# Down projection of the second feed-forward block: from one per pair of tiles to seven block products behind all tiles, in a decoder layer on one core

## The reference

```python
def swiglu(x, w_gate, w_up, w_down):
    return (jax.nn.silu(x @ w_gate) * (x @ w_up)) @ w_down

    h = swiglu(rmsnorm(x, ffn1_pre_norm[i]), ffn1_w_gate[i], ffn1_w_up[i], ffn1_w_down[i])
    x = x + MACARON_WEIGHT * rmsnorm(h, ffn1_post_norm[i])
    h = hybrid_mixer(rmsnorm(x, mix_pre_norm[i]), cos, sin, w_in[i], conv_w[i], conv_b[i],
                     dt_bias[i], a_log[i], d_skip[i], ssm_norm[i], w_out[i])
    x = x + rmsnorm(h, mix_post_norm[i])
    h = swiglu(rmsnorm(x, ffn2_pre_norm[i]), ffn2_w_gate[i], ffn2_w_up[i], ffn2_w_down[i])
    x = x + MACARON_WEIGHT * rmsnorm(h, ffn2_post_norm[i])
```

## Time and profile before

| | |
|---|---|
| median of three runs | 2281.05 us |
| lowest and highest of the three | 2279.21 and 2282.74 us |
| span of the profiled execution | 2278.5 us |
| TensorE busy in it | 2238.8 us, 98% |
| VectorE busy | 1698.9 us, 75% |
| ScalarE busy | 917.6 us, 40% |
| GpSimd busy | 230.4 us, 10% |

### The profile page before, as it was taken

How to read it: one execution, slowest core, us unless ns; L and a number is a source line. 1 busy time by engine, 2 the same in 40 slices (tenths; PEclk the granted TensorE clock), 3 DMA queues, 4 the chain that set the end, 5 groups by cost and what they waited for, 6 DMA issues and landing times. The chain is left out here.

```text
span 2278.5 us, 29774 instructions
## 1 busy us (share of the span) xinstructions
PE 2238.8 (98%) x10460; PEld 1835.5 (81%) x10460; DVE 1698.9 (75%) x2547; ACT 917.6 (40%) x1614; POOL 230.4 (10%) x213
## 2 busy tenths in 40 slices
PE   9999999999999999999999999999999999999998
PEld 7888888888877877778788777788888888888887
DVE  8877777777759787786666686879877777777767
ACT  6322222222334576777531774225332222222224
POOL 0000000000000344443100226100000000000000
PEclk9999999999999999999999999999999999999999
DMA  4111111111323001101221135133121111111123
GB/s 161 56 51 47 50 55 55 55 50 38 124 100 114 20 10 38 38 10 56 75 67 54 65 121 175 56 121 111 38 70 50 47 55 55 55 55 52 41 87 135
DMA packets 54748, 154.65 MB, mean 68 GB/s; under 512 B 6144, under 2 KB 8192, under 8 KB 52608
## 3 DMA queue, kind: packets, MB, share of 16 engines
q1 hardware_dynamic: 54656, 153.46, 20.0%
HBM read 132.14 MB, written 21.30 MB: 67 GB/s over the span
## 5 line engine op out<-in xcount | busy, mean ns | idle before, releaser
L1094 DVE TENSOR_TENSOR acc<-psum,acc 128x512 f32<-128x512 f32 x288 | 197.8, 690 | 161.0 <-PE psum L583 158.2
L710 ACT CAST t_hi<-t_raw 128x512 fp32r<-128x512 f32 x144 | 89.6, 622 | 319.9 <-DVE t_raw L900 303.0
L583 PE MATMUL psum<-act_hi,tile_lo 128*128 128x512 f32 x544 | 211.9, 389 | 0.0
L582 PE MATMUL psum<-act_lo,tile_hi 128*128 128x512 f32 x544 | 211.9, 389 | 0.0
L581 PE MATMUL psum<-act_hi,tile_hi 128*128 128x512 f32 x544 | 211.9, 389 | 0.0
L732 ACT ACTIVATE sum<-sum 128x512 f32<-128x512 f32 x72 | 45.6, 633 | 245.1 <-DVE sum L1048 150.4
L2097 PE MATMUL psum<-norm_hi,tile_hi 128*128 128x512 f32 x320 | 129.2, 404 | 1.8 <-DVE z_scaled L2505 1.8
L2414 DVE TENSOR_TENSOR probs_t_lo<-psum,probs_t_hi 128x512 fp32r<-128x512 f32 x144 | 97.1, 685 | 39.2 <-ACT probs_t_hi L2331 38.3
L2099 PE MATMUL psum<-norm_hi,tile_lo 128*128 128x512 f32 x320 | 125.1, 391 | 0.0
L2098 PE MATMUL psum<-norm_lo,tile_hi 128*128 128x512 f32 x320 | 125.0, 391 | 0.0
L581 PEld LDWEIGHTS psum<-act_hi,tile_hi 128*128 128x128 f32 x544 | 102.2, 188 | 21.2
(11 more groups left out here) (436 smaller groups left out, 5870.2 us busy)
## 6 DMA issues: line engine op xcount, KB each, us to landing
tile_lo_raw<-in_d SPq DMA_DIRECT2D x40, 512.0 KB, 4.3
gate_raw<-in_gu SPq DMA_DIRECT2D x36, 512.0 KB, 3.8
up_raw<-in_gu SPq DMA_DIRECT2D x72, 256.0 KB, 3.7
raw_tile<-in_w_att SPq DMA_DIRECT2D x28, 512.0 KB, 3.7
x_scratch<-acc SPq DMA_DIRECT2D x32, 256.0 KB, 2.1
cum_rows<-cum_scratch SPq DMA_DIRECT2D x8, 1024.0 KB, 4.7
raw_tile<-in_w_out SPq DMA_DIRECT2D x15, 512.0 KB, 3.6
gate_up_lo_raw<-in_gu SPq DMA_DIRECT2D x7, 1024.0 KB, 6.1
```

The lines of the kernel that those rows point to most:

```text
L582: pe.matmul(o, w_h[:, s, d, :], a_l[:, s, x], start=False, stop=False)
L583: mm = pe.matmul(o, w_l[:, s, d, :], a_h[:, s, x], start=False, stop=(s == 1))
L710: act.copy(to, of).then_inc(sem(p + "_t_hi"), 1)
L1094: v.tensor_tensor(x, banks(4 + d % 4), x, ALU.add).then_inc(sem(p + "_acc"), 1)
```

## The change

Only the second block changes. The first two tiles stay plain; all 20 others become seven tiles, where the last two were plain. No tile pair has a down projection behind it. The product silu(gate) x up of a tile goes to a staging buffer (`stage`), from there by a 512 KB store to a DRAM scratch (`acts`), 22 times.

Behind all tiles, the whole down projection is one 2x2 block product: the 22 inner tiles in two groups of 11 (rows 0 to 10 and 11 to 21), the 8 output blocks in two groups of 4, with the two token halves on the other side. Seven products (0 to 6 in the code) x 11 steps x 4 blocks x 3 = 924 matmuls. A step is 12 matmuls. The activations come back from DRAM in nine transfers, the weights by steps in 256 KB transfers, two where a product's weights are a sum. GpSimd forms the weight sums (`down_w_sum`, 55 of 128x512, for products 0, 1, 3, 4 and 6), VectorE the activation sums (`down_b_sum`, 55, products 1, 2, 3, 5 and 6), ScalarE the casts `w_hi` and `b_hi`, VectorE the rests `w_lo` and `b_lo` (77 of each). There are 11 slots of operands; slot k is free for product m once TensorE is through step k of product m-1. ScalarE puts 16 results into `down_sums`, VectorE adds 32. The norm and the residual behind it stay; their steps and those of the products are ordered by a new `end_plan`.

```diff
             wait(pe, p + "_up", 4)
             seven_pe(pe, p, 1, 0, sums=True)
             seven_pe(pe, p, 1, 1)
+            if p == "f2":
+                with pe.Fori(2, LAST_PAIR + 1) as i:
+                    seven_pe(pe, p, i, 0)
+                    seven_pe(pe, p, i, 1)
+                return
...
-                v.tensor_tensor(e1[:], e1[:], e4[:], ALU.mult).then_inc(sem(p + "_read"), 1)
+                if p == "f2":
+                    v.wait_ge(sem("act_out"), 16 * (2 * i + s))
+                v.tensor_tensor(stage[0][:, half(0)] if p == "f2" else e1[:], e1[:], e4[:], ALU.mult)\
+                 .then_inc(sem(p + "_read"), 1)
...
+        def down_slot(eng, m, k):
+            if m and k < FG - 1:
+                wait(eng, "dn_step", (FG - 1) * (m - 1) + k + 1)
...
+        def down_start_sp(sp, store):
...
+            down_w_in(sp, 0, 7)
+            down_w_in(sp, 0, 8)
+            store(LAST_PAIR, 1)
+            down_w_in(sp, 0, 10)
+            down_w_in(sp, 0, 9)
+            down_rows_in(sp, 1, half(1), 2, "dn_b_second2")
...
+                if m == 0 and k == 9:
+                    act.wait_ge(sem("act_out"), 16 * FT)
+                elif m == 0 and k == 10:
+                    wait(act, "f2_read", at_tile(LAST_PAIR, 1, 11, 11))
...
+        def down_three(pe, m, k, d):
+            o = banks((0 if m % 2 else 4) + d)
+            pe.matmul(o, dw_hi[k][:, d, :], db_hi[k][:], start=(k == 0), stop=False)
+            pe.matmul(o, dw_hi[k][:, d, :], db_lo[k][:], start=False, stop=False)
+            return pe.matmul(o, dw_lo[k][:, d, :], db_hi[k][:], start=False, stop=(k == FG - 1))
...
+                        if len(DOWN_W[m]) > 1:
+                            add("POOL", "w", ("w_sum", m, k), 1.45, w)
+                            w = ("w_sum", m, k)
+                        add("ACT", "w", ("w_hi", m, k), 0.63, w)
+                        add("DVE", "w", ("w_lo", m, k), 0.69, ("w_hi", m, k))
...
+            rank |= {("DVE", "add"): 1, ("ACT", "put"): 1, ("DVE", "w"): 2, ("DVE", "b"): 2, ("DVE", "b_sum"): 2, ("ACT", "w"): 2,
+                     ("ACT", "b"): 2, ("DVE", "a_sum"): 3, ("DVE", "resid"): 4, ("DVE", "scale"): 5, ("POOL", "w"): 2,
...
-            for h in range(NH2):
-                for d in range(KT):
-                    add("PE", "main", ("down", h, d), 1.36, ("act_lo", 2 * h + 1), ("d_lo", 1),
```

More of the change, by code:

```diff
@@ L345, in pair_of @@
             return tile_of(pairs[:, s % 2], i)
+        LAST_PAIR = FG - 1
         def g_in_sp(sp, p, tile):
@@ L1298, in build, with w_loads, w_sums, b_sums @@
         RSTD_RANK = {(x, "rstd"): 0 for x in ("PE", "ACT", "DVE")}
+        GROUPS_OF_ROWS = ((0, 4), (4, 8), (8, FG))
+        def w_loads(m):
+            return sum(min(len(x), 2) for x in DOWN_W[:m + 1])
+        def w_sums(m, k):
+            return FG * sum(len(x) > 1 for x in DOWN_W[:m]) + k + 1
+        def b_sums(m, k):
+            same = [n for n in range(m) if len(DOWN_B[n]) > 1 and (n in POOL_B) == (m in POOL_B)]
+            return FG * len(same) + k + 1
+        def puts_to(m, d):
+            return sum(u[:2] <= (m, d) for u in PUTS)
@@ new lines, in sums_to, with down_last, down_b, down_b_summed @@
+        def sums_to(m, d):
+            return sum(u[:2] <= (m, d) for u in SUMS)
+        def down_last(h, d):
+            return max(n + 1 for n, u in enumerate(SUMS) if u[1:] == (d % 4, d // 4, h))
+        def down_b(block, k):
+            return b_rows[block[0]][:, k, half(block[1])]
+        def down_b_summed(eng, m, k):
+            wait(eng, "dn_b_sum_pool" if m in POOL_B else "dn_b_sum", b_sums(m, k))
+        def down_slot(eng, m, k):
+            if m and k < FG - 1:
+                wait(eng, "dn_step", (FG - 1) * (m - 1) + k + 1)
+            elif m:
+                wait(eng, "dn_mm", 4 * m)
+            elif DOWN_FREE[k]:
+                wait(eng, "f2_seven", at_tile(LAST_PAIR, 1, 7, DOWN_FREE[k]))
@@ new lines, in down_w_sum, with down_b_sum @@
+        def down_w_sum(g, m, k):
+            wait(g, f"dn_w_in{k}", 16 * w_loads(m))
+            g.tensor_tensor(dw_raw[k][:], dw_raw[k][:], dw_two[k][:], DOWN_W[m][2]).then_inc(sem("dn_w_sum"), 1)
+        def down_b_sum(eng, m, k):
+            down_loaded(eng, m, k)
+            down_slot(eng, m, k)
+            one, two, op = DOWN_B[m]
+            eng.tensor_tensor(db_raw[k][:], down_b(one, k), down_b(two, k), op)\
+               .then_inc(sem("dn_b_sum_pool" if m in POOL_B else "dn_b_sum"), 1)
@@ new lines, in down_product_pe @@
+        def down_product_pe(pe, m, k):
+            last = m == DOWN_N - 1
+            if k == FG:
+                down_bank_free(pe, m, 3)
+                for n in range(FG):
+                    mm = down_three(pe, m, n, 3)
+                mm.then_inc(sem("dn_mm"), 1)
+                return
+            wait(pe, "dn_w_lo", FG * m + k + 1)
+            wait(pe, "dn_b_lo", FG * m + k + 1)
+            for d in range(3 if last else 4):
+                if k == 0:
+                    down_bank_free(pe, m, d)
+                mm = down_three(pe, m, k, d)
+                if k == FG - 1:
+                    mm.then_inc(sem("dn_mm"), 1)
+            if k < FG - 1:
+                mm.then_inc(sem("dn_step"), 1)
@@ new lines, in down_put, with down_add @@
+        def down_put(act, m, d, out, h):
+            sign = {u[:2]: u[2] for u in PUT_OF[m]}[out, h]
+            if m == 4:
+                wait(act, "dn_sum", sums_to(m, d))
+            wait(act, "dn_mm", 4 * m + d + 1)
+            act.activation(dsum[:, 4 * out + d, half(h)], banks((0 if m % 2 else 4) + d), ACT.Copy, scale=sign)\
+               .then_inc(sem("dn_put"), 1)
+        def down_add(v, m, d, out, h):
+            op = {u[:2]: u[2] for u in SUM_OF[m]}[out, h]
+            wait(v, "dn_mm", 4 * m + d + 1)
+            if m == 1:
+                wait(v, "dn_put", puts_to(m, d))
+            n = SUMS.index((m, d, out, h))
+            before = [i + 1 for i, u in enumerate(SUMS[:n]) if u[1:] == (d, out, h)]
+            if before:
+                wait(v, "dn_sum", before[-1])
+            else:
+                wait(v, "dn_put", [u[1:] for u in PUTS].index((d, out, h)) + 1)
+            x = dsum[:, 4 * out + d, half(h)]
+            v.tensor_tensor(x, x, banks((0 if m % 2 else 4) + d), op).then_inc(sem("dn_sum"), 1)
@@ L1731, in turn_half_dve @@
                 v.tensor_tensor(x, banks(4 + d % 4), x, ALU.add).then_inc(sem("wo_acc"), 1)
-            elif step in ("gate", "up", "prod", "act_lo"):
+            elif step in ("gate", "up", "prod"):
                 u = e[0]
@@ L3070, in _ @@
             for step, *e in END["DVE"]:
-                if step in LATE_STEPS:
+                if step == "w_lo":
+                    down_w_lo(v, *e)
+                elif step == "b_sum":
+                    down_b_sum(v, *e)
+                elif step == "b_lo":
+                    down_b_lo(v, *e)
+                elif step == "add":
+                    down_add(v, *e)
+                elif step in LATE_STEPS:
                     late_dve(v, step, e)
@@ L3079, in _ @@
             gate_pool(g)
+            for k in range(EARLY):
+                down_w_sum(g, 0, k)
+            for step, *e in END["POOL"]:
+                if step == "w_sum":
+                    down_w_sum(g, *e)
+                else:
+                    down_b_sum(g, *e)
 def shape_constants():
```

435 lines of the change are left out of this document (326 added, 109 removed).

## The result

The changed kernel took 2287.07 us (median of 8 runs, 2283.88 to 2288.95), before took 2281.16 us beside it (8 runs, 2278.12 to 2283.27). The ratio is 1.0022, 95% interval 1.0012 to 1.0032: slower by 0.2%. The forecast was 2277.6, a gain of 3.4 us. The measured time lies inside the range of 2267 to 2293, but on the other side of before: past the 2285.6 from which the prediction counts the change as slower.

The account below looks back on a forecast made before the run. TensorE's matmuls were taken as the bound: -35.4 saved + 7.6 turn + 1.6 clock + 26.1 before product 6 + 1.6 clock - 4.7 small matmuls and waits - 0.3 tail = -3.4; span 2275.1, plus 2.5 for timed runs: 2277.6 us, range 2267 to 2293.

Parts of the forecast that it names:

- What was saved: Behind round 3: 156 fewer matmuls at 0.2266 us each, 35.4 us saved.
- The turn: Between round 3 and the first seven tile: TensorE waits 7.6 us for `up_lo`, plus 1.6 us at the lower clock.
- The tiles: The 20 seven tiles: 19.04 us each, 380.7 us in all, without waits, the stores costed at nothing.
- Product 6 at t + 205.6: Start of the last down-projection product, t being product 0's start: 26.1 us over the bare matmuls.
- the 12th operation of VectorE: In product 0: VectorE's 12th operation ends at t + 13.6, delayed by the last activation's store, casts and hand-overs.
- the port: Down-projection products: GpSimd's 46 weight sums hold up VectorE's operations with two SBUF inputs, 46.8 us in all.
- the 238th operation: VectorE's last sum (`a_sum` 7, first half) that TensorE's column sums need before product 6; forecast to end at t + 200.7.
- the chain from the seventh sum to product 6: Ahead of product 6: column sums, root, reciprocal, diagonal, broadcast, copy and the first matmul, 4.9 us.
- VectorE falling behind: Rival, products: slower operations, all sums blocking; product 6 at t + 218.8, decided past t + 213.6; 2290.8 us, chance 0.18.
- The other rival: Products: VectorE keeps up because the port costs little; product 6 at t + 198.2, time 2270.2 us, chance 0.20.
- The signs: Products 1 to 5: TensorE waits for `w_lo` or `b_lo`; the forecast is wrong if TensorE is whole there.
- The second sign: Products: forecast wrong if GpSimd's sums stretch well over 1.3 us and `w_hi` comes late because of them.

Follow-up runs that it names:

- e3: Changed kernel with VectorE's order at the turn altered: weight sums and the tile's first two rests ahead of the wide rests; 2283.21 us, ratio to before 1.0014.
- e4: Changed kernel with product 0's start reordered: last activations ahead of steps 1 and 2's operands, early weight casts ahead of late activation casts; 2285.71 us, ratio to before 1.0030.
- e2: Changed kernel with GpSimd's 55 weight sums on one column in place of 512 (output not the reference's); 2277.80 us, ratio to before 0.9989.
- e1: Changed kernel with planner ranks putting the first half's sums of squares and squares before product 6's preparations; 2267.39 us, ratio to before 0.9945.
- e10: Changed kernel with 44 of 55 weight sums (products 1, 3, 4, 6) moved from GpSimd to VectorE; 2284.96 us, ratio to before 1.0025.
- e5: Changed kernel with the ranks of e1 and the start order of e4 together; 2269.32 us, ratio to before 0.9953.
- e7: e5 plus e3's turn order, and TensorE's column sums three steps later in product 5; 2261.07 us, ratio to before 0.9916.
- e9: e7 with 44 of 55 weight sums (products 1, 3, 4, 6) moved from GpSimd to VectorE; 2265.23 us, ratio to before 0.9939.

## Why the prediction was wrong, by its own steps

**What was saved** held: 156 matmuls fewer, TensorE 28.8 us less busy although more of its work ran at the lower clock.

**The turn** held: 7.6 us of hole were forecast, released by `up_lo`, and 7.6 came (1631.5 to 1639.1), and the matmuls behind it take 0.77 and 0.63 us where they take 0.39 at full clock. From `up_lo`'s first product to product 0 it was 383.1 us against 382.3. e3 shows that the size is one of order.

**Not in the sum: the rounds ahead of the turn.** From round 0's first matmul to round 3's end before took 68.5 us (1566.3 to 1634.8) and the changed kernel 65.3 (1566.2 to 1631.5), 3.2 us faster at the better clock of the windows above. (Round 0's first matmul stands at 1566.3, not near 1590 as the section on time before has it.) I had costed the steps taken out there (`act_hi`, `act_lo`, `d_hi`, `d_lo`) at nothing. The other profile of before gave 68.5 again. But seven profiles have the changed kernel's own code in these rounds, and they gave 63.8 (e4), 65.3 and 65.4 (the changed kernel), 65.4 (e2), 66.9 (e1 and e10) and 68.5 (e5), the last as long as before. So one code moves by 4.7 us here from one execution to the next, and that the change makes the rounds faster isn't shown. In the sum below these 3.2 us are luck: without them the profiled span would have been some 9 us over before's, which is what the stretches show (653.0 against 643.9).

**The tiles** held: no waits, a granted clock of 1.00 from 1700 to 2000, the stores in time.

**Product 6 at t + 205.6: this step failed.** It started at t + 216.8, 11.2 us later, past the decision point of t + 213.6 that I had given the slower rival. Three terms of it were too small.

First, the 12th operation of VectorE, forecast at t + 13.6. VectorE's timeline around the last activations:

```profile
2021.63 1.77 DVE L1508 TENSOR_TENSOR down_w_lo<-down_w_raw,down_w_hi 128x512 fp32r<-128x512 f32 x1
2023.33 1.77 DVE L1513 TENSOR_TENSOR down_b_lo<-act_first_rows,down_b_hi 128x512 fp32r<-128x512 f32 x1
2025.02 1.78 DVE L1508 TENSOR_TENSOR down_w_lo<-down_w_raw,down_w_hi 128x512 fp32r<-128x512 f32 x1
...
2030.72 0.68 DVE L1172 TENSOR_TENSOR act_stage<-up,sum 128x512 f32<-128x512 f32 x1
...
2039.64 1.28 DVE L1508 TENSOR_TENSOR down_w_lo<-down_w_raw,down_w_hi 128x512 fp32r<-128x512 f32 x2
```

I had the last activation leave VectorE at t + 3.6 and the store landed at t + 9. But of the early operands that stood ahead of it four were held up beside GpSimd's first sums to 1.77 us each, so that it left at t + 9.2, 5.6 us late. e2, with small sums, had it at t + 4.5: 4.7 of the 5.6 are the hold-up. The store then took 5.3 us, where I had 5.1 (2.5 for the loads ahead of it and 2.6 to land); this agreement is luck, since the same store took 9.4 in e2, behind full transfer engines that my four loads don't account for. The 12th operation ended at 2040.9, t + 18.7: 5.1 us late (e2: t + 17.6). I had weighed the port only for the stretch behind this point. My terms as printed also come to t + 12.7 and not to 13.6 (9, 1.8, 0.7 and 1.2).

Second, from there to the 238th operation (2232.9, t + 210.7): 192.0 us against 187.1. The port cost 41.4 us, less than my 46.8 (e2); the waits for ScalarE and for slots were 11 us where I had put 3, and a rest of 2 us stays unexplained. The port's size was right to 12%; the waits were the term that was too small.

Third, the chain from the seventh sum to product 6: 6.1 us against 4.9. TensorE's part ran at the lower clock, which I had charged only behind the hole: 1.84 us for the column sums and 2.08 for the broadcast, where before's trace has 0.95 and 1.02 at full clock. The 4.9 was misread, too: the interval from 1612.17 starts with the root, so the column sums aren't in it, while the broadcast's turn behind other matmuls is.

**Product 6 itself** took 32.6 us to the first transposed block, against 31.5. **The tail** behind it was 12.7 us, 0.9 less than before's 13.6 where I had 0.3 less.

Together, against my sum: -3.2 (rounds), +0.8 (tiles), +11.2 (start of product 6), +1.1 (product 6), -0.6 (tail): 9.3 us, which leads from 3.4 faster to 5.8 slower. The rival that was named for it, VectorE falling behind with every sum blocking in full, has the right place and nearly the right time of product 6 (t + 218.8), but not the cause: the port cost less than forecast, and the lateness is 5.1 us of start, 4.9 of waits (less what the port cost under its price) and 1.2 of chain. (The other rival's t + 198.2 adds up to 197.8 from its terms. e2, where the sums cost nearly nothing, is its case: product 6 at t + 204.5, because product 0 alone lost 10.5 us where I had 5.)

**The signs.** The prediction named TensorE's waits for `w_lo` or `b_lo` through products 1 to 5, and called itself wrong if TensorE was whole there, "the port is cheap". It was whole: each of the five products took 29.9 or 30.0 us, without a wait. Yet the port wasn't cheap, 41.4 us. VectorE stayed ahead of TensorE in all operands of these products and was behind only at the one operation for which the column sums wait. So the sign was badly chosen, and it didn't tell the port's cost from the order's. The second sign came as well: GpSimd's sums took 1.61 us on average. Whether `w_hi` came late by it isn't shown, since VectorE waited for it 6.3 us in the changed kernel and 8.1 in e2.

**The port's rule.** By the Trainium skill, "SBUF — State Buffer", section "Who interferes with whom", a VectorE instruction with two SBUF inputs contends with a GpSimd instruction that reads SBUF, and one SBUF input doesn't. The runs agree: 0.965 against 0.683 us for two inputs, 0.678 against 0.679 with one in PSUM. Blocking in full by each of 46 sums would have been 59.3 us; measured are 41.4.

**What I did not see at all** is that the largest term was not a price but an order. The forecast took it as given that TensorE must wait at the column sums; in e1 the seventh sum was made at t + 176.9 in place of t + 210.7, and the stretch was 20 us shorter.

## What to carry to other kernels

When a scheduler places a small chain (here four column sums and a broadcast) ahead of a long run of matmuls on the busiest engine, look for what the chain's last input stands behind on the other engine: two ranks gave back 20 us, more than any other repair of the order (6.4 for the turn, 2.7 for the start of product 0). A planner that doesn't know of hold-ups between engines can then place such steps too early (e5), and a place that suits one order may not suit the next (e7 against e9). Where work is taken off the bounding engine, add up the second engine over the whole stretch, from its first late instruction on: once it binds, savings on the first engine turn into waits (e4, e5). Check what a sign of being wrong would look like under each rival, and profile one kernel more than once before a few us at another clock are put down to a change.
